# The last output tile of a gated convolution layer, finished in pieces of 256, 128 and 128 columns instead of 256 and 256

## The reference, cut to what matters

```python
hn = rms_norm(x, norm_g)
a, b, gate = jnp.split(hn @ w_in, 3, axis=-1)
u = a * jax.nn.sigmoid(b)
u = depthwise_causal_conv(u, conv_w) + conv_b
u = layer_norm(u, ln_g, ln_b)
u = jax.nn.silu(u) * jax.nn.silu(gate)
return x + u @ w_out
```

## Time and profile before

| what | value |
|---|---|
| median of the runs | 370.73 us (370.05 to 371.03) |
| the profiled execution's own time | 370.11 us |
| span of its trace | 368.0 us |
| TensorE, share of the span busy | 99% |
| VectorE | 86% |
| GpSimd | 74% |
| ScalarE | 57% |
| share of TensorE in the chain that ended last | 97% |
| from the start of the last add to the end of the span | 2.7 us |

### The profile page before, as it was taken

One profiled execution on the slowest core, in us unless ns is written; L12 is line 12 of the kernel. 1 busy time (PEld: TensorE's weight loads), 2 busy tenths in 40 slices (PEclk: granted clock), 3 DMA queues, 4 the chain that ended last, 5 costly groups with the idle time before them and its releaser, 6 DMA issues.

```text
span 368.0 us, 4866 instructions
## 1 busy us (share of the span) xinstructions
PE 363.2 (99%) x1632; PEld 296.3 (81%) x1632; DVE 317.3 (86%) x505; ACT 208.2 (57%) x317; POOL 273.8 (74%) x195
## 2 busy tenths in 40 slices
PE   7999999999999999999999999999999999999997
PEld 6888888888888888888888888888888888888886
DVE  4758799999999899998999999963789999996942
ACT  6979685568537632874666657643436971342400
POOL 0127999999999995999999999996676543458310
PEclk9999999999999999999999999999999999999999
DMA  7995011301111011111011110113313596064042
GB/s 268 399 406 190 19 57 57 113 4 57 57 59 57 2 59 57 57 59 38 19 61 57 57 55 5 57 59 110 118 59 115 183 391 226 2 229 172 30 161 97
DMA packets 13705, 39.33 MB, mean 107 GB/s; under 512 B 1520, under 2 KB 2032, under 8 KB 13680
## 3 DMA queue, kind: packets, MB, share of 16 engines
q1 hardware_dynamic: 13536, 38.87, 29.0%
q10 hardware_dynamic: 144, 0.15, 0.2%
HBM read 34.82 MB, written 4.19 MB: 106 GB/s over the span
## 4 chain that ended last, share of the span: by engine, by line
PE 97%; DMA 1%; SPq 0%; ACT 0%; DVE 0%; issue 0%
PE mm L580 67%; PE acc L675 12%; PE mm L675 9%; PE mm L597 6%; PE mm L648 2%; DMA nat<-x_t 1%; PE acc L666 0%; PE acc L656 0%; PE acc L574 0%; SPq L481 0%; ACT x_hi L745 0%; DVE nat L1196 0%; SPq L469 0%
## 5 line engine op out<-in xcount | busy, mean ns | idle before, releaser
L580 PE MATMUL mm<-x_hi,w_hi 128*128 128x512 f32 x352 | 139.9, 397 | 0.0
L580 PE MATMUL mm<-x_hi,w_lo 128*128 128x512 f32 x352 | 138.9, 395 | 0.0
L580 PE MATMUL mm<-x_lo,w_hi 128*128 128x512 f32 x352 | 138.8, 394 | 0.0
L1108 DVE SCALAR_TENSOR_TENSOR acc<-u,chan,acc 128x512 f32<-128x512 f32 x154 | 108.3, 748 | 0.1
L580 PEld LDWEIGHTS mm<-x_hi,w_lo 128*128 128x128 f32 x352 | 66.3, 188 | 15.4
L580 PEld LDWEIGHTS mm<-x_lo,w_hi 128*128 128x128 f32 x352 | 66.4, 189 | 15.0
L580 PEld LDWEIGHTS mm<-x_hi,w_hi 128*128 128x128 f32 x352 | 66.4, 189 | 14.9
L1408 POOL TENSOR_TENSOR pconv<-pconv,prod 128x512 f32<-128x512 f32 x60 | 76.8, 1302 | 0.0
L1108 DVE SCALAR_TENSOR_TENSOR acc<-u,w_sum,acc 128x512 f32<-128x512 f32 x90 | 67.3, 748 | 0.2
L834 ACT ACTIVATE prod<-u,chan 128x512 f32<-128x512 f32 x73 | 50.6, 718 | 16.0 <-POOL pconv L1408 12.8
L1352 POOL TENSOR_TENSOR w_lo<-raw,w_hi 128x1024 fp32r<-128x1024 f32 x21 | 50.6, 2410 | 8.1 <-ACT w_hi L784 8.0
(11 more groups left out here) (102 smaller groups left out, 526.0 us busy)
## 6 DMA issues: line engine op xcount, KB each, us to landing
raw<-w_in SPq DMA_DIRECT2D x22, 512.0 KB, 3.2
nat<-x_t SPq DMA_DIRECT2D x16, 256.0 KB, 5.9
sgate<-x SPq DMA_DIRECT2D x8, 512.0 KB, 11.3
raw<-w_out SPq DMA_DIRECT2D x8, 512.0 KB, 3.3
nat<-x SPq DMA_DIRECT2D x8, 512.0 KB, 9.1
y<-nat SPq DMA_DIRECT2D x15, 256.0 KB, 2.1
raw_late<-w_out SPq DMA_DIRECT2D x4, 512.0 KB, 3.8
sig<-w_out SPq DMA_DIRECT2D x4, 512.0 KB, 3.7
```

The costliest lines, as they stand in the source:

```text
L580: ins = nc.tensor.matmul(bank(("unit", m, h)), w[:, m % 3, k, :], xx[:, k, half(h)], start=(k == 0 and i == 0), stop=(k == KC - 1 and i == 2))
L1108: ins = nc.vector.scalar_tensor_tensor(dst, chain_in(j, chain, k), tap(j, chain, k), chain_bank(j, chain), ALU.mult, ALU.add)
```

## The change

A table `TAIL` gives the pieces of the last row tile: columns 0 to 256, 256 to 384 and 384 to 512. The last product now has pieces q = 3, 4 and 5. Each is 12 matmuls, an add and a store. The banks are those that product 4 used for its row tiles 0, 1 and 2: `acc` 0, `acc` 1 and a bank of `mm`.

```diff
+TAIL = ((0, 256), (256, 384), (384, 512))
+LAST_Q = 2 + len(TAIL)
-POSTS = [(b, part, q) for b in (1, 0, 2, 3, 4, 5, 6) for q in range(4 + (b == 6))
+POSTS = [(b, part, q) for b in (1, 0, 2, 3, 4, 5, 6) for q in range(LAST_Q + 1 if b == 6 else 4)
...
             if b == 6 and q >= TPH - 1:
-                return acc[:, q - TPH + 1, 0:HALF // 2]
+                columns = piece_columns(b, q)
+                return product_bank(4, q - TPH + 1)[:, 0:columns.stop - columns.start]
...
-            return CONTINUES.get(b) if (b, q) not in ((6, TPH - 1), (6, TPH)) else None
+            return CONTINUES.get(b) if b < 6 or q < TPH - 1 else None
...
             if b == 6 and q >= TPH - 1:
-                return slice(HALF // 2 * (q - TPH + 1), HALF // 2 * (q - TPH + 2))
+                return slice(*TAIL[q - TPH + 1])
...
-            for q in range(TPH + 1):
+            for q in range(LAST_Q + 1):
                 sp.wait_ge(post_done, POST[6, "12", q])
                 store("12", min(q, TPH - 1), piece_columns(6, q))
-            sp.wait_ge(y_out, 16 * (NH * NT + 1))
+            sp.wait_ge(y_out, 16 * (NH * NT + len(TAIL) - 1))
...
-                for q in range(TPH + (b == 6)):
+                for q in range(LAST_Q + 1 if b == 6 else TPH):
...
-            def posts(b, columns=range(TPH + 1)):
+            def posts(b, columns=range(LAST_Q + 1)):
```

## The result

The changed kernel took 371.41 us, the median of 14 runs (371.07 to 372.78), beside 370.37 us for the kernel before in runs of the same series (370.05 to 371.03). The ratio is 1.0028, with a 95% interval of 1.0021 to 1.0035: +1.04 us, from +0.78 to +1.30. The interval leaves out 1, so the runs do tell the two kernels apart. The 0.28% itself lies inside the 0.3% that the prediction had called the bound; the interval reaches over it. The span of the profiled execution is 369.0 us, +1.0. A comparison by difference has to start at the last tile, though, since the two traces do not reach it at the same moment: its first matmul starts at 362.42 now and at 362.22 before.

A forecast was written before the change was run, and what follows sets the result against it. TensorE, busy for 363.2 of 368.0 us, was taken to bound the kernel. The terms +1.23 - 0.01 - 0.13 - 0.10 gave +0.99 us, 371.7 us beside the median of 370.73; range 370.4 to 372.5.

The forecast's parts named there:

- the bound: Whole kernel's time: within 0.3%, or 1.11 us, a measurement can't tell a change from none.
- last matmul's start, TensorE: Last tile: 24 matmuls of 128 columns replace 12 of 256, so the last starts at 366.18 against 364.95, +1.23 us.
- the last add: Last tile's final add on VectorE: 128 columns for 256, 0.29 us for 0.42, -0.13 us.
- The step: Narrow matmuls of the last tile: 0.11 us each, a load of 128 columns not hidden; near ends 0.062 and 0.119.
- The first rival: Last tile's narrow matmuls: load hidden wholly or in part; wholly, step 0.062, sum -0.14 us, 370.6 us; chance 0.15.
- its milder form: Last tile's narrow matmuls: load partly hidden, about 81 ns a pair, sum +0.3 us; within the 0.15 chance.
- The second: Last tile: narrow fp32r handled like plain float32, two records and 0.22 us a matmul, +3.7 us, 374.4; chance 0.12.
- The third: End of the kernel: middle add or store overlaps the last ones and becomes the end; no price; chance 0.03 with remainder.
- The way through the array: From the last matmul's start to its add: 0.06 us less by columns, 0.01 by records; taken as -0.01.
- The store: Last store, rows of 512 bytes for 1 KB: saves between nothing and 0.25 us, taken as -0.10 us.
- The chances: Outcome of the whole kernel's time: faster 0.03, same 0.60, slower 0.37.

The follow-up runs named there:

- The half operand: Changed kernel with its two narrow pieces using 64 of the tile's 128 rows as stationary operand; one execution of 370.33 us.
- four pieces: Changed kernel with the last tile in four pieces of 128 columns; ratio 1.0055 to the kernel before.
- 384 and 128: Changed kernel with the last tile in pieces of 384 and 128 columns; ratio 0.9999 to the kernel before.
- one piece: Changed kernel with the last tile in one piece of 512 columns, nothing split; ratio 1.0008 to the kernel before.
- one store: Changed kernel with its last two pieces stored together, 128 KB behind the last add; ratio 1.0036 to the kernel before.
- split add: Matmuls of the kernel before, last piece added in two halves of 128 columns, the second stored by ScalarE; ratio 0.9994 to the kernel before.
- two queues: Kernel before with its last store split into two of 64 KB, issued by SyncE and ScalarE; ratio 1.0003 to the kernel before.
- the one at 365.26: Matmuls of the kernel before, last add in two halves, both stores issued by SyncE; one execution of 373.24 us.
- 320 and 192 columns: Changed kernel with the last tile in pieces of 320 and 192 columns; one execution of 370.39 us, beside 370.65 for the kernel before.
- both split adds: Kernel before with the last add in two halves: second half stored by ScalarE, ratio 0.9994; both stored by SyncE, one execution of 373.24 us.
- 64 columns: Changed kernel with the last tile in pieces of 256, 128, 64 and 64 columns; one execution of 372.41 us.

## Why the prediction was right

The prediction was +0.99 us and 371.7; measured were +1.04 and 371.41. Set against the medians the forecast holds, and so does its mechanism: the narrow matmuls pay for their loads, and what is saved behind them is less. That the sum came within 0.05 us is in part luck. The tile explains +0.80 us; the saving of the store was put 0.18 us too low, and 0.24 us of the timed difference that no term of the prediction holds made up for it. The same goes for the span of 369.0, which was forecast and measured: 0.20 of it stands ahead of the tile. The difference of 0.3 in the absolute time is the base, whose median fell from 370.73 over three runs to 370.37 over fourteen. By its terms, in the tile:

| term | predicted | measured |
|---|---|---|
| last matmul's start, TensorE | +1.23 | +1.21 (2.51 for 1.30) |
| from there to the add | -0.01 | 0.00 (0.32, 0.32) |
| the last add | -0.13 | -0.13 (0.29 for 0.42) |
| from the add's end to the end of the span | -0.10 | -0.28 (2.03 for 2.31) |
| sum | +0.99 | +0.80 |

*The step.* 0.11 was taken from a gap between two loads at the start of the program and from the transposes, and 0.111 came out. The error of 0.02 in the term is the first step, which the prediction priced like the others and which is 0.06, since the load for the next matmul could start with it at once. The half operand shows that the load is what sets the step: this was an inference before and is an experiment now. One of the grounds given for it was none: the load side's 1.43 of 1.45 us in the earlier trace rows says only that the records of the loads overlap. The widths settle what the prediction left between 0.11 and 0.119: from 512, 384 and 320 columns the line runs on to 0.119 at 256, so that step is still set by the columns.

*The first rival* (the load hidden) is refuted by the steps, and so is its milder form, a load hidden in part: with fp32r operands and a full stationary operand every step of 64, 128 and 192 columns took 0.11 us, but for the first step of a piece behind a wider one (0.06 to 0.09). The Trainium skill's page "TensorE: Matmul & The Clock Gate" gives 81 ns for a load and a 128-column matmul in "Back-to-back issue gap"; this case measured 0.111 us. One slip in the prediction changes no price: by its own terms SyncE would have been free for 0.4 us ahead of the last store in this rival's case, not for 0.2. *The second* (narrow fp32r treated like plain float32) would have left 48 records and 0.22 a matmul; there are 24, at 0.111. *The third* found nothing: the middle add was over 1.05 us before the last one, and joining the stores made the tile longer.

*The way through the array.* By its columns a 128-wide matmul would be 0.06 shorter; it stayed at 0.32 us to the add. With the half operand it was 0.26 (365.61 to 365.87, with records of 0.22). The first narrow matmul of the changed kernel, at 363.85, has a record of 0.22 as well, and those behind it, which start 0.06 us after their load does, have 0.27 or 0.28. So behind a load that sets the step this way doesn't shrink with the columns; the transposes' 272 ns had told as much.

*The store* is the term that was mis-sized: 0.28 for 0.10. The prediction set bounds, nothing and 0.25, and gave no reason for the value that it took between them; the upper one was the nearer, and even that was passed, by less than the rounding of the span. The landing time doesn't fall evenly with the size. In the traces the last stores took 1.5 us for 32 KB, 1.6 or 1.7 for 64 KB (1.9 for one of two at once), 1.8 for 96 KB, 1.9 for 128 KB and 2.0 for 256 KB. The DMA engines show where it is saved. Both times they stand still for 0.78 us behind the issue. Then they work from 366.50 to 367.10 before and from 367.78 to 368.20 after. That is 0.18 us less; the remaining 0.1 lies between the last bytes and the end of the span. Before, then after:

```profile
366.50:367.10 0.60, 0.00 (x0) 0.00 (x0) 0.00 (x0) 0.00 (x0) 0.00 (x0) 1.00 0.65 219
```
```profile
367.78:368.20 0.42, 0.00 (x0) 0.00 (x0) 0.00 (x0) 0.00 (x0) 0.00 (x0) 0.50 0.54 156
```

*What stays open.* The tile gives +0.80 us and the timed ratio +1.04, with +0.78 to +1.30. For the other timed kernels the pairs (tile, time) are +2.09 and +2.0 (four pieces), +0.16 and 0.0 (384 and 128), +0.37 and +0.3 (one piece), +1.01 and +1.3 (one store), -0.12 and -0.2 (split add), +0.11 and +0.1 (two queues). The differences have both signs and stay within the intervals. (The times are those of the ratios. The medians of the runs lie 1.7 us apart for four pieces and 1.1 for one store, so these two are not known better than that.) The traces reach the tile anywhere from 362.22 to 363.25, without the one at 365.26, and the kernel before has the earliest of them. The chain that ended last shows where the 0.20 us ahead of the tile come from in the changed kernel's trace: not from the start of the program, after which it is 0.10 us ahead, but from two stretches of the input projection, in code that the change does not touch. Before, then after:

```profile
38.53 45.31 PE mm L580 x195
...
84.71 36.25 PE mm L580 x156
```
```profile
38.43 45.49 PE mm L583 x195
...
84.79 36.40 PE mm L583 x156
```

Together they take 81.56 us before and 81.89 after, and every other trace has one of these two lengths to within 0.01. The longer one stands also in the traces of 320 and 192 columns, of the single last store and of both split adds; the shorter one in all others, those of four pieces and of 64 columns among them. So it does not go with the number of pieces. Whether it belongs to a build of the kernel or to a single execution can't be told from one trace each, and so the 0.24 stays open.

*The chances.* 0.60 for no change and 0.37 for slower fit a result at 0.28% with an interval that reaches over 0.3%. What did not hold is the statement that within 0.3% a measurement can't tell a change from none: the interval measured here leaves it out.

## What to carry to other kernels

Splitting the last tile shortens the add and the store behind it, but each piece brings its own loads of the stationary operand, and a piece narrower than what a load takes pays for the load: here 0.111 us a step for 64, 128 and 192 columns of fp32r, where 256 took 0.119. In the tile two halves were worth 0.4 us over one piece of 512, and the third piece cost 0.8 us. If shorter adds and stores are wanted beyond that, split the add and the store and leave the matmuls as wide as their load; here this gave 0.12 us in the tile and nothing that the times can show. A change at the end of a long program is best read from its first touched instruction to the end of the span, since what lies ahead of it differs between traces by as much as the change is worth.

## What the runs showed of the hardware that was not expected

Two adds of 128 x 128 out of PSUM that follow each other without a wait took 0.49 us together, though each alone takes 0.29: the second one cost 0.20. A store of 64 KB in rows of 512 bytes landed sooner (1.6 us) than one of 128 KB in rows of 1 KB (1.9): no penalty for the shorter rows was seen. TensorE's granted clock, 1.00 through the work, stood at 0.50, which is 1.2 GHz, from 367.4 on in the changed kernel; TensorE had its last matmul at 366.36 and nothing to do after it, so this cost nothing. In the run whose first load came 1.27 us late, the same level cost 1.5 us, since TensorE had work then.
